# A mixture-of-experts decoder step on one core: down products over every eighth weight column, sums kept in natural column order

## The reference, cut to what matters

```python
xp = xp + mix @ w_out[l]                      # the same for xs
h_all = concatenate([_rms(xp, norm2_g[l]).reshape(B * S, D), _rms(xs, norm2_g[l]).reshape(DB * QS, D)])
y_all = _moe(h_all, w_router[l], b_router[l], w_up[l], b_up[l], w_down[l], b_down[l])
xp = xp + y_all[:B * S].reshape(B, S, D)      # the same for xs: the outputs

# in _moe, for the rows of one expert e:
up = xblk @ w_up[e] + b_up[e]
x_glu = minimum(up[..., :D_FF], 7.0)
x_lin = clip(up[..., D_FF:], -7.0, 7.0)
act = x_glu * sigmoid(1.702 * x_glu) * (x_lin + 1.0)
y = (act @ w_down[e] + b_down[e]) * gate      # added to the row of its token
```

## Time and profile before

| | us |
|---|---|
| median of three runs | 2768.79 (2763.79 to 2775.37) |
| span of the profiled execution | 2770.9 |
| TensorE busy | 2572.2 (93%) |
| weight loads of TensorE | 2121.2 (77%) |
| VectorE, ScalarE, GpSimd busy | 935.0, 640.0, 489.8 |
| up passes, down passes of the experts | 1008.1, 507.8 |
| mean granted clock of TensorE | 0.959 |

### The profile page before, as it was taken

One profiled execution on the slowest core, in us unless ns is written; L12 is line 12 of the kernel. 1 busy time (PEld: TensorE's weight loads), 2 busy tenths in 40 slices (PEclk: granted clock), 3 DMA queues, 4 the chain that ended last, 5 costly groups with the idle time before them and its releaser, 6 DMA issues.

```text
span 2770.9 us, 44569 instructions
## 1 busy us (share of the span) xinstructions
PE 2572.2 (93%) x18128; PEld 2121.2 (77%) x18128; DVE 935.0 (34%) x2614; ACT 640.0 (23%) x1621; POOL 489.8 (18%) x476
## 2 busy tenths in 40 slices
PE   7999978989988869939999999999999999999994
PEld 3555536445665635439999999999999999999994
DVE  1132234217756434442422222223232232322321
ACT  1111122217756412211111111111111111111111
POOL 0000021100000101231322312313132331222211
PEclk9999987999999989969999999999999999999997
DMA  5000044213000252157777887988898999989994
GB/s 195 16 23 14 21 127 117 41 44 137 1 1 1 90 172 87 66 172 254 255 266 264 261 284 265 303 296 287 312 302 311 333 307 331 315 308 326 312 331 152
DMA packets 282018, 533.64 MB, mean 193 GB/s; under 512 B 52546, under 2 KB 93474, under 8 KB 281602
## 3 DMA queue, kind: packets, MB, share of 16 engines
q1 hardware_dynamic: 234818, 474.38, 48.3%
q0 software_dynamic: 33504, 46.98, 8.0%
q10 hardware_dynamic: 13488, 9.37, 1.1%
HBM read 492.21 MB, written 42.96 MB: 193 GB/s over the span
## 4 chain that ended last, share of the span: by engine, by line
PE 54%; DMA 1%; POOL 0%; issue 0%; SPq 0%; DVE 0%; POOLq 0%; ACT 0%; DVEq 0%; ACTq 0%
PE up L2233 36%; PE down L2244 18%; DMA w_up<-summed_rows 1%; DMA slot_rows<-slot_tokens_gates 0%; POOL x_rows L2191 0%; DMA summed_rows<-y_rows,row_index_cur 0%; SPq L2181 0%; POOL summed_rows L2197 0%; DMA x_rows<-h_rows,row_index_cur 0%; PE down L2250 0%; POOLq L2077 0%; ACT y_rows L2263 0%; DVEq L2142 0%; DVE w_down L2428 0%; ACTq L2285 0%
## 5 line engine op out<-in xcount | busy, mean ns | idle before, releaser
L2233 PE MATMUL up<-hT,w_up 128*128 128x128 f32 (+19 forms) x8192 | 1008.1, 286 | 12.1 <-DVE hT L2322 12.1
L2233 PEld LDWEIGHTS up<-hT,w_up 128*128 128x128 f32 x8192 | 1005.0, 191 | 12.4 <-issue 12.4
L2244 PE MATMUL down<-actT,w_down 128*128 128x128 f32 (+19 forms) x4096 | 507.8, 286 | 0.0
L2244 PEld LDWEIGHTS down<-actT,w_down 128*128 128x128 f32 x4096 | 503.6, 191 | 1.1
L2197 POOL DMA_INDIRECT summed_rows<-y_rows,row_index_cur x153 | 241.3, 1577 | 1085.0 <-ACT y_rows L2263 1048.4
L2342 DVE TENSOR_SCALAR glu<-up,b_up_cur 128x128 f32<-128x128 f32 (+19 forms) x256 | 93.6, 366 | 1000.4 <-PE up L2233 1000.4
L352 PE MATMUL zp<-w_in,xnT 128*128 128x512 f32 (+1 forms) x800 | 321.6, 558 | 1.4 <-DVE xnT L567 1.4
L2274 ACT ACTIVATE sig<-glu 128x128 f32<-128x128 f32 (+19 forms) x256 | 82.4, 322 | 862.6 <-DVE glu L2342 862.6
L352 PEld LDWEIGHTS zp<-w_in,xnT 128*128 128x128 f32 x800 | 144.7, 196 | 156.2 <-issue 152.8
L2282 ACT ACTIVATE yT<-down,b_down_cur 128x128 f32<-128x128 f32 (+19 forms) x256 | 97.2, 380 | 394.4 <-PE down L2244 394.4
L2191 POOL DMA_INDIRECT x_rows<-h_rows,row_index_cur x153 | 149.3, 976 | 59.7 <-issue 46.0
(11 more groups left out here) (412 smaller groups left out, 1958.2 us busy)
## 6 DMA issues: line engine op xcount, KB each, us to landing
w_up<-in_w_up SPq DMA_DIRECT2D x128, 2048.0 KB, 13.2
w_down<-in_w_down SPq DMA_DIRECT2D x64, 2048.0 KB, 12.4
w_in<-in_w_in SPq DMA_DIRECT2D x5, 2048.0 KB, 13.1
x<-in_x_prompt SPq DMA_DIRECT2D x8, 512.0 KB, 3.6
window_rows<-in_x_prompt SPq DMA_DIRECT2D x8, 512.0 KB, 3.9
summed_rows<-cache_rows SPq DMA_DIRECT2D x8, 512.0 KB, 2.7
h_rows<-h SPq DMA_DIRECT2D x8, 512.0 KB, 3.6
w_up<-summed_rows SPq DMA_DIRECT2D x8, 512.0 KB, 8.9
```

The source lines that it names most:

```text
L2233: mm = nc.tensor.matmul(up[c % 2][:, h, :N], U[c // 4][:, h, kk, w0:w0 + P], hT[:, kk, :N], start=(kk == 0), stop=(kk == KC - 1))
L2244: mm = nc.tensor.matmul(dn[d % 2][:, :N], Dn[:, kk // 4, kk % 4, d * P:d * P + P], aT[:, kk, :N], start=(kk == 0), stop=(kk == KC - 1))
```

## The change

It does four things. The stationary of down chunk d is every eighth column of the weights, starting at d: columns d, d + 8, d + 16 and so on. Then `yT[m, d]` is column 8m + d, and quarter b of a row, written by `give_y` as (j, d) instead of (c, j), is simply columns 256b to 256b + 255: `acc_dram` is in natural order. x2 is stored in natural order too. h stays in quarters: the gain multiply, now a product of its own ahead of the norm's scalar, writes h in that order, and ScalarE scales it afterwards; the square goes to a buffer of its own. The bias of the down products is loaded directly in its new order, in 4096 pieces of 32 bytes. At the end SP copies `acc_dram` to the outputs in DRAM, in five copies.

```diff
@@ phase_out @@
-        gain = k.qT[:, 3, 0:D]
+        squares = sb("squares_e", [P, D])
+        s_hg, s_inv = sem("h_gained"), sem("e_root_inverted")
-        by_quarter = lambda ap: ap.rearrange("p (c b j) -> p b c j", b=4, c=KC)
-        parts = lambda ap: ap.rearrange("p (b c j) -> p b c j", b=4, c=KC)
+        by_part = lambda ap: ap.rearrange("p (b c j) -> p c b j", b=4, c=KC)
...
                     pe.wait_ge(s_b, 32)
-                    for m in range(6):
+                    for m in range(4):
                         mm = nc.tensor.transpose(tp[m // 4][:, m % 4, :], braw[:, m, :], C[:, at["ident"]])
...
             act.dma_start(braw[:, 0:4, :], bup).then_inc(s_b, 16)
-            act.dma_start(braw[:, 4:6, :], bdn).then_inc(s_b, 16)
+            with nc.allow_non_contiguous_dma(reason="bias of the down products by column of its chunk"):
+                act.dma_start(k.bdT[:].rearrange("p (e d) -> p e d", d=KC), i["b_down"][0].rearrange("e (p d) -> p e d", d=KC)).then_inc(s_b, 16)
             for t in range(NT):
                 R = rows(t)
                 act.wait_ge(s_x2, t + 1)
-                if t >= 2:
-                    act.wait_ge(s_st[t % 2], 32 * (t // 2))
-                nc.scalar.activation(h[t % 2][:R, :], x2[t % 2][:R, :], ACT.Square, accum_out=ss[:R, t:t + 1]).then_inc(s_ss, 1)
+                nc.scalar.activation(squares[:R, :], x2[t % 2][:R, :], ACT.Square, accum_out=ss[:R, t:t + 1]).then_inc(s_ss, 1)
                 act.wait_ge(s_ms, t + 1)
                 nc.scalar.activation(ss[:R, 2 * NT + t:2 * NT + t + 1], ss[:R, NT + t:NT + t + 1], ACT.Sqrt).then_inc(s_rt, 1)
+                act.wait_ge(s_hg, t + 1)
+                act.wait_ge(s_inv, t + 1)
+                nc.scalar.activation(h[t % 2][:R, :], h[t % 2][:R, :], ACT.Copy, scale=ss[:R, 3 * NT + t:3 * NT + t + 1]).then_inc(s_h, 1)
                 evict(t)
...
                 for n in range(2):
-                    half = xx[:R].rearrange("p (b y c j) -> p y c b j", b=4, y=2, c=4)[:, n]
-                    last = V.tensor_tensor(half, blocks(op[t % 2][n][:R, :]), blocks(x[t % 2][:R, n * 512:n * 512 + 512]), ALU.add)
+                    half = slice(n * 512, n * 512 + 512)
+                    last = V.tensor_tensor(xx[:R, half], op[t % 2][n][:R, :], x[t % 2][:R, half], ALU.add)
                 last.then_inc(s_x2, 1)
+                dve.wait_ge(s_x2, t + 1)
+                if t == 0:
+                    dve.wait_ge(s_g, 160)
+                V.tensor_tensor(by_part(hh[:R]), blocks(xx[:R]), blocks(g2[:R]), ALU.mult).then_inc(s_hg, 1)
                 dve.wait_ge(s_ss, t + 1)
                 V.tensor_scalar(ss[:R, NT + t:NT + t + 1], ss[:R, t:t + 1], 1.0 / D, EPS, ALU.mult, ALU.add).then_inc(s_ms, 1)
                 dve.wait_ge(s_rt, t + 1)
-                link(V.reciprocal(ss[:R, 3 * NT + t:3 * NT + t + 1], ss[:R, 2 * NT + t:2 * NT + t + 1]))
-                if t == 0:
-                    dve.wait_ge(s_g, 160)
-                    link(V.tensor_copy(parts(gain), by_quarter(g2)))
-                V.scalar_tensor_tensor(out=hh[:R, :], in0=xx[:R, :], scalar=ss[:R, 3 * NT + t:3 * NT + t + 1],
-                                       in1=gain[:R], op0=ALU.mult, op1=ALU.mult).then_inc(s_h, 1)
+                V.reciprocal(ss[:R, 3 * NT + t:3 * NT + t + 1], ss[:R, 2 * NT + t:2 * NT + t + 1]).then_inc(s_inv, 1)
@@ phase_experts @@
+        every_eighth = lambda ap: ap.rearrange("p (m d) -> p d m", d=KC)
...
-            for t in ORDER:
-                sp.dma_start(summed[t][:rows(t)], k.acc_dram[t * P:t * P + rows(t), :]).then_inc(s_l[t], 16)
-            sp.wait_ge(s_st, 16 * NT)
+            sp.dma_start(k.o["xs"].rearrange("b s d -> (b s) d"), k.acc_dram[S:T, :]).then_inc(s_st, 16)
+            for n in range(4):
+                part = slice(n * S // 4, (n + 1) * S // 4)
+                sp.dma_start(k.o["xp"][0, part, :], k.acc_dram[part, :]).then_inc(s_st, 16)
+            sp.wait_ge(s_st, 16 * 5)
...
-                        mm = nc.tensor.matmul(dn[d % 2][:, :N], Dn[:, kk // 4, kk % 4, d * P:d * P + P], aT[:, kk, :N],
+                        mm = nc.tensor.matmul(dn[d % 2][:, :N], every_eighth(Dn[:, kk // 4, kk % 4])[:, d], aT[:, kk, :N],
                                               start=(kk == 0), stop=(kk == KC - 1))
...
-                if m % 2 == 1:
-                    act.wait_ge(s_l[t], 16)
-                    nc.scalar.copy(in_order(natural[t][:R]), stored(summed[t][:R])).then_inc(s_nat[1], 1)
-                act.wait_ge(s_nat[m % 2], m // 2 + 1)
-                act.dma_start(dst, natural[t][:R]).then_inc(s_st, 16)
...
-                    V.transpose(ysb[:, a, :].rearrange("p (c j) -> p c j", c=KC), yT[:, :, 32 * a:32 * a + 32]).then_inc(s_yr, 1)
+                    V.transpose(ysb[:, a, :].rearrange("p (j d) -> p d j", d=KC), yT[:, :, 32 * a:32 * a + 32]).then_inc(s_yr, 1)
...
-            for m, t in enumerate(ORDER):
-                if m % 2 == 0:
-                    R = rows(t)
-                    dve.wait_ge(s_l[t], 16)
-                    V.tensor_copy(in_order(natural[t][:R]), stored(summed[t][:R])).then_inc(s_nat[0], 1)
```

More of the change, by code:

```diff
@@ L1791, in phase_out @@
         g2, br = k.qT[:, 0, 0:D], k.qT[:, 1, 0:NE]
-        gain = k.qT[:, 3, 0:D]
+        squares = sb("squares_e", [P, D])
         x2 = [k.nat[:].rearrange("p b s x -> p (b s x)")[:, 4096 + D * j:4096 + D * j + D] for j in range(2)]
-        braw = k.qT[:, 1, NE:NE + 6 * P].rearrange("p (m x) -> p m x", m=6)
+        braw = k.qT[:, 1, NE:NE + 4 * P].rearrange("p (m x) -> p m x", m=4)
         h = [sb(f"h{j}", [P, D]) for j in range(2)]
@@ L1947, in _ @@
             bup = i["b_up"][0].rearrange("e (c p) -> (e c) p", p=P).rearrange("(t r) p -> r t p", r=P)
-            bdn = i["b_down"][0].rearrange("e (c p) -> (e c) p", p=P).rearrange("(t r) p -> r t p", r=P)
             act.dma_start(braw[:, 0:4, :], bup).then_inc(s_b, 16)
-            act.dma_start(braw[:, 4:6, :], bdn).then_inc(s_b, 16)
+            with nc.allow_non_contiguous_dma(reason="bias of the down products by column of its chunk"):
+                act.dma_start(k.bdT[:].rearrange("p (e d) -> p e d", d=KC), i["b_down"][0].rearrange("e (p d) -> p e d", d=KC)).then_inc(s_b, 16)
             for t in range(NT):
@@ L2046, in _ @@
                     dve.wait_ge(s_bt, 1)
-                    V.tensor_copy(k.buT[:], tp[0][:].rearrange("p a b -> p (a b)"))
-                    V.tensor_copy(k.bdT[:], tp[1][:, 0:2, :].rearrange("p a b -> p (a b)")).then_inc(s_bc, 1)
+                    V.tensor_copy(k.buT[:], tp[0][:].rearrange("p a b -> p (a b)")).then_inc(s_bc, 1)
                     dve.wait_ge(s_bc, 1)
@@ L2108, in phase_experts @@
         s_carry, s_dc = sem("wait_carrier"), sem("experts_dve_chain")
-        s_l, s_nat, s_st = [sem(f"summed_loaded{t}") for t in range(NT)], [sem(f"rows_in_order_{n}") for n in ("dve", "act")], sem("outputs_stored")
+        s_st = sem("outputs_stored")
         block = ctx.enter_context(nc.Block())
@@ L2299, in _ @@
             overflow(act, block_body)
-            for m, t in enumerate(ORDER):
-                R = rows(t)
-                dst = k.o["xp"][0, t * P:t * P + P, :] if t < PT else k.o["xs"].rearrange("b s d -> (b s) d")
-                if m % 2 == 1:
-                    act.wait_ge(s_l[t], 16)
-                    nc.scalar.copy(in_order(natural[t][:R]), stored(summed[t][:R])).then_inc(s_nat[1], 1)
-                act.wait_ge(s_nat[m % 2], m // 2 + 1)
-                act.dma_start(dst, natural[t][:R]).then_inc(s_st, 16)
         @block.vector
```

## The result

| | before | after |
|---|---|---|
| median, us (runs) | 2766.4 (4, 2763.79 to 2775.37) | 3237.62 (4, 3233.19 to 3242.63) |
| span of the profiled execution, us | 2770.9 | 3233.4 |
| down passes, us | 507.8 | 983.4 |
| up passes, us | 1008.1 | 1006.6 |
| mean granted clock | 0.959 | 0.966 |

The ratio is 1.1684, 95% interval 1.1654 to 1.1714. With a fourth execution the median of the kernel before is 2766.4 us instead of 2768.8. The forecast was 3135 in a range of 2745 to 3175: direction and cause came out as forecast, the size lies above the range.

The account below looks back on a forecast made before the run. TensorE was taken to bound the expert stage without waits, paced by the longer of weight load and product. Median 2768.8 + 380.2 (part 1) - 13.8 (parts 2 to 5) = 3135 us, range 2745 to 3175.

Parts of the forecast that it names:

- 1. The stationary: Down products: 4096 strided weight loads at 217 ns a pass, 888.0 us against 507.8, +380.2; +411 at the write's price.
- +3: Down pass estimate: 3 ns that a pass at the load's floor takes beyond its 109.3 ns column time.
- The lower working (192 ns): Down passes: the reduction's extra 0.63 ns an element on top of the load's 0.854, 192 ns a pass, +280 us.
- 2. The tail: Kernel's end: five DRAM-to-DRAM copies move 4.33 MB once at 420 GB/s, -12.6 us; -6.2 at 260 GB/s.
- 0.3: Tail: the 0.3 us added after 2.1 us and 10.3 us of data to reach the end at 2758.3.
- 3. The stage before the experts: Before the experts: scaling moved to ScalarE saves 1.2 us after the last tile, two fewer bias transposes 0.27; together -1.4.
- 4. The bias load: Down bias on ScalarE's queue: 4096 pieces land in about 9 us, with 6 us of cover, so no cost.
- 5. The transposes of y: Expert stage, VectorE: strided writes take 595 ns instead of 409, hidden except for the last expert's first, +0.2 us.
- Load free: Rival for the down products: the weight load doesn't pay for the stride, part 1 is 0, 2755 us; chance 0.25.
- Half: Rival for the down products: load at one and a half times its column time, 167 ns, +176, 2931 us; chance 0.05.
- The clock: Rival for the down products: granted clock also falls to 1.2 GHz, mean pass 245 ns, +496, 3251 us; chance 0.04.
- Few DMA engines: Rival for the tail: copies run on one DMA engine, 133 us, +123, 2878 with a free load; chance 0.02.

Follow-up runs that it names:

- columns map: Kernel before, with the down products' stationary at stride 1 or 8 elements and 128, 96, 64 or 32 columns, varied by chunk: 2946.0 us.
- tail alone: Kernel before with only the tail changed, SP copying the summed rows from DRAM to the outputs: ratio 0.9971, -8.0 us.
- the stage alone: Kernel before with only the changed stage before the experts, its expert stage and tail as before: ratio 0.9987, -3.6 us.

## Why the prediction was right or wrong

What bounds the kernel: held. No wait appeared in the stage, and the down line's +475.6 us is the expert stage's +474.1. Of what was to be seen, the passes of one length whatever their width, the untouched up line, the clock at 1.00 and the lower DMA share (0.71 instead of 0.93) are there; the load's record is 336 ns instead of about 300.

1. The stationary. The mechanism held, the size did not: forecast 217 ns a pass and +380.2 us, measured 240 ns and +475.6; even the upper bound, +411, was too low. The step that failed is the term "+3" in "128 x 1.67 + 3". The price of a lone element, taken from a VectorE reduction, was right: the columns map gives 1.66 ns. But the fixed part was carried over from contiguous loads, where 3 ns stand beyond the column time; a load at stride 8 has some 22 to 27. At 128 x 1.66 + 27 = 239 ns a pass the working would have given 4096 x 0.240 = 983 us. The bounds missed it because both ends, 1.67 and 1.73, varied the price of an element and neither varied the fixed part. The reduction's own 152 ns of fixed time in the earlier trace rows could have warned that a slope and an intercept are two unknowns, and that a slope borrowed from another engine says nothing of the intercept. One thing stays open: the reduction read elements 128 bytes apart, 32 elements, and at that stride the load took 219 ns, close to the 217 forecast. Columns were varied at stride 8 only, so no run shows how the 219 splits, nor why stride 8 costs 20 ns more. The lower working (192 ns) took the extra per element on top of the load's own time; it is out as well.

2. The tail: forecast -12.6, measured -7.9 in the trace and -8.0 (-12.2 to -4.2) alone. The data came near the forecast: they ended between 12.4 us (tail alone) and 14.0 us (kernel after) behind SP's first copy, against 12.4 for the forecast's 2.1 + 10.3. What failed for the larger part is the "0.3" behind them: the span ended 3.9 and 3.4 us after the last data. The tail before showed 1.6 us there (its last data at 2769.3, span end 2770.9).

3. The stage before the experts: forecast -1.4, traced about -2 in all three kernels that have it (and -3.6, -6.7 to -0.8, by the times of the stage alone). The order held: in the kernel after ScalarE's scaling of the last tile begins at 1177.82, right behind VectorE's reciprocal, and VectorE's queue goes on at once. Scaling a tile took ScalarE 1.15 us, not 1.04.

4. The bias load: landed after 13.4 us (issued 1012.84), forecast about 9, and it was wanted at 1027.8. The cover shrank from the forecast 6 us to 1.6 but held: nothing, as forecast.

5. The transposes of y: 624 ns, forecast 595, from 409; hidden.

Sum of 2 to 5: forecast -13.8, measured with the contiguous stationary -13.6 (-18 to -9). That the two agree to 0.2 us is luck: the tail gave some 4.6 less than forecast, the stage made up 0.6 to 2.2 of it, and the rest is within the interval.

The rivals. Load free: its condition, a pace under 112 ns, isn't met, and the rule it rested on, the LDWEIGHTS section of the Trainium skill ("TensorE: Matmul & The Clock Gate"), gives 107 ns for what took 240; for neighbours the trace agrees with it, and at stride 2 nothing speaks against it. Its price for the rest, the same -13.8, stands beside the -13.6 above: 2755 forecast, 2762.5 and 2764.3 measured with a contiguous stationary, where the kernel before took 2774.5 and 2773.4. Half: no. The clock: 3251 is the forecast nearest to the time, 3237.6, and still wrong, so its nearness is chance: the clock stayed at 1.00; twice the passes of before would be 224 ns at 128 columns and 300 at 176, and both are 240. Few DMA engines: the share in the tail went up to 1.24.

The range failed with the term: it left room above 3135 for an element's price only. 3237.6 - 3135 = 102.6, of which 95.4 is part 1 and 4.7 the tail; the remaining 2.5 is less than the spread of the kernel after's own four times.

## What to carry to other kernels

A product whose passes are short (here 128 to 176 f32 columns) is soon overtaken by its weight load. A stationary whose f32 elements lie 32 bytes apart made a pass 2.1 times as long at 128 columns and 1.6 times at 176; 8 bytes apart was free, and so was the 32-byte stride of the stationary behind 512 moving columns, whose passes last 439 ns (a strided moving operand of that length was not run). To turn an order around, pay for it in an operation that is hidden (a copy of VectorE, a transpose) or that happens once, not in one that is repeated 4096 times. When a cost is borrowed from another engine, bound the fixed part and the part per element separately, and take the price from the same stride if there is one: here the part per element was right to 0.01 ns and the sum was short by 23.

## What was not expected of the hardware

The prediction spoke of the weight load alone. The moving operand pays for a stride as well (227 to 233 ns for 128 columns at 16 and 32 bytes), and both together cost little more than one.

A stride of 48 bytes costs more than any other tried (267 ns against 216 to 240 for the others from 16 bytes on). Why is open.

In the kernel with 32 moving columns the clock did fall, which it did in no window of the kernel after from 1300 us to the end of its expert stage. Windows of the same expert as above:

```profile
2797.00:2799.00 2.00, 2.00 (x12) 2.00 (x12) 0.00 (x0) 0.24 (x1) 0.00 (x0) 1.00 1.05 385
2799.00:2801.00 2.00, 2.00 (x13) 2.00 (x12) 0.00 (x0) 0.13 (x1) 0.00 (x0) 0.58 1.05 388
2801.00:2803.00 2.00, 2.00 (x14) 1.78 (x13) 0.00 (x0) 0.37 (x1) 0.00 (x0) 0.50 1.05 389
...
2810.00:2815.00 5.00, 5.00 (x47) 5.00 (x47) 1.19 (x4) 0.76 (x4) 0.00 (x0) 1.00 0.76 266
```

From 2795.5 on strided loads of 128 columns served products of 32; soon after 2799 the clock went to 0.50 (1.2 GHz), and the four plain passes at the chunk's end took 1.20 us at 2800.86 instead of 0.69 at 2798.25. Under the next up products it was at 1.00 again. TensorE's busy time is 2.00 of 2.00 us throughout, so it doesn't warn of this. So the clock rival was no idle one, although it missed for the kernel after. A strided load itself doesn't seem to follow the clock: with 64 columns a pass took 133 ns in the columns map, at a clock of 1.00, and 132 here, at 0.50.
